# Four output tiles side by side at four stage entries, from weight blocks of two contraction tiles

## The chip, the core and the metric

The kernel runs on one core of one Trainium2 chip. The metric is the device time of one execution in microseconds (us); lower is better. TensorE (PE in the profile) does the matrix products, ScalarE (ACT) and VectorE (DVE) prepare operands and take results out of the PSUM banks, GpSimd (POOL) adds squares for the norms, and SyncE (SP) issues the DMAs. Each engine works through its own list of instructions in order; semaphores hold an instruction until another engine has done what it needs.

## What is computed

The program is two transformer-like blocks on 256 tokens of width 2048, all in float32. Reduced to its large products (`D = 2048`, `T = 256`):

```python
# first block
u = rmsnorm(x, norm_pre)
proj = u @ a_w_in                      # 2048 -> 4096: first half "xb", second half "gate"
xc = causal_conv4(proj[:, :D]) ; r, i = sigmoid(xc @ w_r), sigmoid(xc @ w_i)       # "gates"
y = (linear_recurrence(r, i, xc) * silu(proj[:, D:])) @ a_w_out                    # "aout"
x1 = x + rmsnorm(y, norm_post)
x2 = x1 + sigmoid(x1 @ ple_w_gate) * (p @ ple_w_proj)                              # "pleg", "plep"
# second block
mod = silu(c) @ w_mod + b_mod          # shifts, scales and gains of the norms
um = rmsnorm(x2) * (1 + sc_m) + sh_m
proj = um @ w_in                       # 2048 -> 11264: "cv","cg","i","ff","fb","q","g","gc","gh"
x3 = x2 + ga_m * rmsnorm(merge(conv_branch, hgrn_branch) @ w_out)                  # "wout"
u2 = rmsnorm(x3) * (1 + sc_f) + sh_f
out = x3 + ga_f * rmsnorm(relu(u2 @ mlp_w1) ** 2 @ mlp_w2)                         # "mlp1", "mlp2"
```

A context of 256 further tokens takes part in `i`, `ff` and `fb`; its normed form `uc` is made by the background task `prepare_ctx`.

## The kernel before, in words

**Layout and products.** Activations lie feature-major: 16 feature tiles of 128 partitions by 256 tokens. An output tile is 128 output features by 256 tokens, summed over the 16 tiles of the contraction (`kt` 0 to 15, called k-tiles here). For precision every weight and every activation is split into a high part of reduced width and the remainder. One product of one k-tile into one output tile is three matmuls (high by high, high by low, low by high; every matmul has the line L758), or two wider ones in `mlp1` and `mlp2`.

**Weight blocks.** Weights come from HBM in blocks of 128 x 1024 float32 (512 KB). A block holds 8 k-tiles of one output tile, so a tile takes two blocks. A DMA puts it in one of 7 buffers `WF`; ScalarE writes the high part to one of 4 buffers `WH` (L1015, 128x1024); VectorE writes the low part, `WF` minus `WH`, to `WL` (L1377, 128x1024). ScalarE may overwrite a slot only when PE has done the last product of the block four earlier (semaphore `prod`).

**Order.** `timetable()` writes out one list of steps, and every engine walks that list and does its share of each step. `prepare()` puts the `split` steps (WH, WL) so that PE has them `LA` = 2 blocks ahead. `linear()` runs one output tile: for each half `begin()` (which calls `prepare()`), eight products; then `evac`, in which ScalarE and, for some kinds, VectorE take the tile out of its bank. Four PSUM banks (`GBANKS` = 4) go round; the first product into a bank waits until it was freed (semaphores `free0` to `free3`). Steps of `background` tasks are put between products by `tick()`.

**Stage entries.** At the start of `xb`, `pleg`, `cv` and `mlp1` the activations themselves are only being made: step `make` has VectorE scale one k-tile, ScalarE write its high part and VectorE its low part (L1384 and L1377, 128x256), for `pleg` two k-tiles at a time (128x512). There `linear_pair()` runs two output tiles side by side, so that each k-tile serves both as it appears. Its two tiles need four blocks, in the order first half of both, second half of both. `make` runs some four k-tiles ahead of the products.

**Fills.** The modulation product `mod` (192 blocks, 24 column groups of 8) is spread over the kernel: `modp` steps do it on PE (four 128x512 matmuls a block, line `bank<-WF,SM`), `modv` steps on VectorE (L1384, 128x512). Some `modp` blocks stand before an entry, so that PE has work while a norm is being finished. `close` and `row` steps bring the sums into place.

Of the kernel before, what the change touches and what calls it, by code (L numbers as in the profile page):

```python
# [13 lines left out]
P = 128  # L14
# [41 lines left out]
def timetable():  # L56
# [26 lines left out]

    def add_pair(kind, name, one, two, fill=(0, 0, 0), after=0):


        order.append((kind, (one, two)))
        cg, kp0, kp1 = fill
        ring = [{"of": "w", "name": name, "index": index, "lo": lo} for lo in (0, BLK) for index in (one, two)]
# [4 lines left out]
    add_pair("xb", "a_in", 0, 1)  # L94
    for j in range(1, 8):
        for n in range(2):
            add("xb", "a_in", 2 * j + n)
            if j > 1 or n:
                add_spread()
        if j % 2 == 0:  # L100
            add("gates", "a_gates", j // 2 - 1)
# [9 lines left out]
    for j in range(4):  # L111
        add("plep", "ple_p", j, (0,))
    add_pair("pleg", "ple_g", 0, 1, (1, 0, 8), 4)
    for j in range(2, 16):
        add("pleg", "ple_g", j)
        add_mod(j % 2, 64)
    add_pair("cv", "w_in", 40, 41, (20, 0, 4), 2)
    for t in range(42, 56):
        add("cv" if t < 48 else "cg", "w_in", t)
        add_mod(int(t < 48), 160)  # L120
    for t in range(24):
# [20 lines left out]
    for q in range(4):  # L142
        if q == 0:
            add_pair("mlp1", "mlp1", 0, 1, (20, 4, 8))
        for j in range(2 if q == 0 else 0, 16):
# [134 lines left out]
    def skip():  # L280
        while blocks[st["at"]]["of"] != "w":
            st["at"] += 1
# [12 lines left out]
    def product(what, n, first=True, last=True):  # L295

        at = len(steps)
        for k in range(n):
            steps.append(("prod", what, k, first and k == 0, last and k == n - 1, k == n - 1, st["used"]))
            if k + 1 < n:  # L300
                tick()
        st["prod"] += 1
        return at
# [18 lines left out]

    def linear_pair(kind, js):
        for j in js:
            new_tile((kind, j))
        made = 0
        for h in range(2):
            while made < min(8 * h + 4, KT):
                steps.append(("make", kind, made))
                made += 1  # L330
            begin()
            for k in range(8):
                while made < min(8 * h + k + 5, KT):
                    steps.append(("make", kind, made))
                    made += 1
                for n, j in enumerate(js):
                    steps.append(("prod", (kind, j, h), k, h + k == 0, h == 1 and k == 7, k == 7, st["used"] + n))
            for n in range(2):
                st["prod"] += 1
                skip()  # L340
                end()
        for n, j in enumerate(js):
            tile[(kind, j)].append(st["prod"] - 1 + n)
            steps.append(("evac", (kind, j)))
            if kind in AFTER:
                chains.append([kind, j, 0])
        advance()
# [5 lines left out]
    for kind, j in order:  # L353
        first = kind not in seen
        if kind == "pleg" and first:
            prepare(ahead=NB - 1)
        if first or (kind == "mlp2" and j[1] == 0):
            settle()
        seen.add(kind)
        pair = isinstance(j, tuple) and kind != "mlp2"  # L360
        if kind == "xb":
            if pair:
# [35 lines left out]
        elif kind == "pleg":  # L398
            if pair:
                prepare(fill=8)  # L400
                linear_pair(kind, j)
            else:
                linear(kind, j)
            if j == 5:
                steps.append(("load_ctx",))
            if j == 15:
                steps.append(("warm", 2))
        elif kind == "cv":
            if pair:
# [5 lines left out]
                linear_pair(kind, j)  # L415
                st["stride"] = 4
            else:
                linear(kind, j)
            if j == 42:
                steps.append(("keep",))  # L420
                background.append(("prepare_ctx", 0))
        elif kind == "cg":
            linear(kind, j - 48)
        elif kind == "i":
            if first:
                finish()
                background.append(("conv_branch", 0))
            linear(kind, j)
        elif kind == "ff":
            linear(kind, j - 8)  # L430
        elif kind == "fb":
            if first:
                while background:
                    step()
                background.append(("ctx_decayed", 0))
            linear(kind, j - 16)
        elif kind == "q":
            if first:
                finish()
                background += [("conv_split", 0), ("ctx_decayed", 1), ("ctx_states", 0)]  # L440
                background += [("hgrn", pr) for pr in range(4)]
                beside += [("readout", pr) for pr in range(4)]
            linear(kind, j - 24)
        elif kind == "g":
            if first:
                while ("ctx_states", 0) not in finished:
                    step()
            linear(kind, j - 32)
        elif kind in ("pw", "hout"):
            if kind == "hout" and first:  # L450
                finish()
            linear(kind, j, 1)
        elif kind in ("gc", "gh"):
            linear(kind, j - (56 if kind == "gc" else 72))
            if kind == "gh" and first:
                steps.append(("back",))
        elif kind == "wout":
            if first:
                mods_done(8, 12)
                steps.append(("gains", "wout"))  # L460
                steps.append(("warm", 3))
            linear(kind, j)
        elif kind == "mlp1":
            if pair:
# [11 lines left out]
                linear_pair(kind, j)  # L476
# [29 lines left out]
def build(nc, ctx, ins, out):  # L506
# [247 lines left out]
    def tensor_program(tensor):  # L754
# [11 lines left out]

        def product(what, k, start, stop, inc, n):
            kind, j, h = what
            slot, kt, off = n % NB, 8 * h + k, k * P
            if kind != "gates":  # L770
# [15 lines left out]
            elif kind == "gates":  # L786
                g, b, ri, m = j
                f = 4 * g + 2 * b + k
                hi, lo, off = XCs[:, f % 8, 0, :], XCs[:, f % 8, 1, :], (ri * 2 + k) * T + m * P
                w.wait_ge(xc_lo, f + 1)  # L790
            elif kind == "aout":
                w.wait_ge(ys_lo, kt + 1)
            elif kind == "plep":
                off = k * 512 + (j % 4) * P
                w.wait_ge(ps_lo, k + 1)
            elif kind == "pleg":
# [212 lines left out]
    def scalar_program(scalar):  # L1009
# [65 lines left out]
        def evac(what):  # L1075
# [295 lines left out]
    def vector_program(vector):  # L1371
# [167 lines left out]
        def after(kind, j, n):  # L1539
# [9 lines left out]
            elif kind == "pleg":  # L1549
                s = area(58 + j % 2, 1)[:, 0, :]  # L1550
                w.wait_ge(*left((kind, j)))
# [427 lines left out]
```

## Time and profile before

| what | us |
|---|---|
| median of 3 runs | 2226.75 |
| range of the 3 runs | 2226.0 to 2229.08 |
| the profiled execution, whole | 2226.39 |
| its span in the profile | 2224.6 |
| PE busy in the span | 2135.6 |
| VectorE busy | 1586.5 |
| ScalarE busy | 988.0 |

The page gives for each engine the time in which it was busy. PE leaves 2224.6 - 2135.6 = 89.0 us of the span unused. The other engines have more free time in all, but they work in order and often stand waiting for each other, and where PE waits it is for one of them. Times inside the trace count from the start of the span; 1.8 us of the execution lie outside it.

### The profile page before, as it was taken

What the parts mean: (1) busy time and instruction counts of PE and PEld (TensorE: products, weight loads), DVE (VectorE), ACT (ScalarE), POOL (GpSimd) and SP (SyncE); (2) the same over time, 40 slices, a digit from 0 to 9 for tenths busy, and PEclk for the clock granted to TensorE, in tenths of its full rate; (3) what the DMA queues carried; (4) which work ended last, traced back from release to release, by engine and by line L of the source; (5) the groups of instructions that cost most, each with busy time, mean ns of one, the idle gap of its engine ahead of it and who ended that gap; (6) DMA issues with size and microseconds to landing.
All of it is one profiled execution on the core that took longest, in us unless ns stands there. A gap on an engine that the chain in (4) does not pass through costs nothing.

```text
span 2224.6 us, 33792 instructions
## 1 busy us (share of the span) xinstructions
PE 2135.6 (96%) x14048; PEld 1915.5 (86%) x14048; DVE 1586.5 (71%) x2365; ACT 988.0 (44%) x1494; POOL 52.3 (2%) x61
## 2 busy tenths in 40 slices
PE   6999989999899999999999999989999999999997
PEld 4778889797898788999989999968888888888886
DVE  7667688688769768657676888866675675655665
ACT  5576444445532322444544444444444434434443
POOL 0000002010000000000000000100000000000000
PEclk9999999999999999999999999999999999999998
DMA  5666768575642457533335988945675685555552
GB/s 199 201 197 201 251 225 274 196 268 195 235 154 95 133 197 232 176 124 123 124 116 160 327 310 300 327 138 194 223 265 199 208 264 189 187 192 189 189 180 95
DMA packets 121689, 447.94 MB, mean 201 GB/s; under 512 B 13504, under 2 KB 13760, under 8 KB 121152
## 3 DMA queue, kind: packets, MB, share of 16 engines
q1 hardware_dynamic: 121536, 445.78, 59.6%
q8 instruction: 111, 1.82, 0.3%
q14 instruction: 42, 0.34, 0.0%
HBM read 441.53 MB, written 4.19 MB: 200 GB/s over the span
## 4 chain that ended last, share of the span: by engine, by line
PE 66%; DVE 6%; ACT 2%; issue 1%; DVEq 0%
PE bank L758 66%; DVE AR L1377 2%; DVE WL L1377 1%; DVE AR L1384 1%; DVE AR L1464 1%; ACT WH L1015 1%; ACT AR L1016 0%; DVE SR L1384 0%; PE bank L879 0%; DVE AR L1380 0%; ACT AR L1015 0%; ACT L1016 0%; PE bank L910 0%; DVE AR L1711 0%; ACT SR L1016 0%
## 5 line engine op out<-in xcount | busy, mean ns | idle before, releaser
L758 PE MATMUL bank<-SR,WH 128*128 128x256 f32 (+1 forms) x8128 | 1945.7, 325 | 44.3 <-DVE WL L1377 25.8
L758 PEld LDWEIGHTS bank<-SR,WH 128*128 128x128 f32 x8128 | 1366.6, 192 | 197.0 <-issue 37.1
L758 PE MATMUL bank<-SR,WL 128*128 128x256 f32 (+1 forms) x5088 | 1481.2, 291 | 0.0
L1377 DVE TENSOR_TENSOR WL<-WF,WH 128x1024 fp32r<-128x1024 f32 x636 | 763.8, 1221 | 354.4 <-ACT WH L1015 353.8
L758 PEld LDWEIGHTS bank<-SR,WL 128*128 128x128 f32 x5088 | 974.9, 192 | 15.1
L1015 ACT ACTIVATE WH<-WF 128x1024 fp32r<-128x1024 f32 x636 | 642.8, 1052 | 118.6 <-PE bank L758 110.8
L1384 DVE SCALAR_TENSOR_TENSOR AR<-WF,SM,AR 128x512 f32<-128x512 f32 x345 | 258.6, 771 | 7.8
L1015 ACT ACTIVATE AR<-bank 128x256 f32<-128x256 f32 (+2 forms) x199 | 80.2, 414 | 263.3 <-PE bank L758 249.9
L1015 ACT ACTIVATE SR<-AR 128x256 fp32r<-128x256 f32 (+1 forms) x154 | 64.6, 427 | 296.4 <-DVE AR L1384 177.6
L1016 ACT ACTIVATE AR<-bank 128x256 f32<-128x256 f32 x152 | 56.1, 380 | 284.9 <-PE bank L758 284.6
L1377 DVE TENSOR_TENSOR AR<-AR 128x256 f32<-128x256 f32 (+7 forms) x376 | 165.2, 474 | 18.8 <-ACT AR L1016 14.7
L1377 DVE TENSOR_TENSOR AR<-AR,bank 128x256 f32<-128x256 f32 x112 | 47.1, 421 | 91.9 <-PE bank L758 65.6
L1903 POOL TENSOR_TENSOR AR<-AR 128x256 f32<-128x256 f32 x56 | 51.9, 927 | 2150.8 <-ACT AR L1016 2150.8
L1016 ACT ACTIVATE AR<-AR 128x256 f32<-128x256 f32 (+3 forms) x70 | 42.9, 614 | 121.3 <-DVE AR L1377 57.8
L758 PE MATMUL bank<-AR 128*128 128x128 f32 (+1 forms) x416 | 66.0, 303 | 12.7 <-ACT AR L1015 9.4
L1384 DVE SCALAR_TENSOR_TENSOR AR<-AR,PR 128x256 f32<-128x256 f32 (+12 forms) x168 | 73.8, 442 | 4.8
L1377 DVE TENSOR_TENSOR SR<-AR,SR 128x256 fp32r<-128x256 f32 (+1 forms) x154 | 65.8, 434 | 14.8 <-ACT SR L1015 14.2
L758 PE MATMUL bank<-WF,SM 128*2 128x512 f32 x160 | 73.4, 592 | 0.0
L758 PEld LDWEIGHTS bank<-AR 128*128 128x128 f32 x416 | 57.1, 195 | 16.3 <-ACT AR L1015 10.8
L1377 DVE TENSOR_TENSOR AR<-bank,AR 128x256 f32<-128x256 f32 x80 | 33.6, 420 | 22.8 <-ACT AR L1016 21.8
L758 PEld LDWEIGHTS bank<-WF,SM 128*2 128x2 f32 x160 | 11.2, 84 | 39.4 <-issue 35.9
L1016 ACT ACT_TABLE_LOAD x32 | 41.1, 1283 | 1.3 <-PEq L1970 0.7
(64 smaller groups left out, 451.7 us busy)
## 6 DMA issues: line engine op xcount, KB each, us to landing
WF<-in_mlp SPq DMA_DIRECT2D x256, 512.0 KB, 4.3
WF<-in_mod SPq DMA_DIRECT2D x192, 512.0 KB, 4.9
WF<-in_w_in SPq DMA_DIRECT2D x176, 512.0 KB, 4.3
WF<-in_a_in SPq DMA_DIRECT2D x64, 512.0 KB, 5.0
WF<-in_a_out SPq DMA_DIRECT2D x32, 512.0 KB, 5.1
WF<-in_ple_g SPq DMA_DIRECT2D x32, 512.0 KB, 5.9
WF<-in_w_out SPq DMA_DIRECT2D x32, 512.0 KB, 5.7
WF<-in_pw SPq DMA_DIRECT2D x16, 512.0 KB, 3.5
```

Source lines behind the costliest of these rows:

```text
L758: return tensor.matmul(o, l, r, start=start, stop=stop, skip_group_check=True)
L1015: return scalar.activation(o, x, f, scale=scale)
L1016: return scalar.activation(o, x, f, scale=scale, bias=bias)
L1377: return vector.tensor_tensor(o, a, b, op)
L1384: return vector.scalar_tensor_tensor(o, a, s, b, op1, op2)
L1464: vector.reciprocal(dst, dst).then_inc(st_rs, 1)
L1903: pool.tensor_tensor(ACC, ACC, SQ[ft % 2], ALU.add).then_inc(acc, 1)
```

## The change

- `linear_pair()` becomes `linear_quad()`: at the four entries output tiles 0 to 3 (40 to 43 of `w_in`) run side by side.
- The weights of these four tiles are laid out anew on the host (`beside`): a block now holds k-tiles 2b and 2b+1 for all four tiles. Eight blocks b = 0 to 7 are consumed in turn, each by 8 products. The total of blocks, products and evacuations is the same.
- `make` now runs two to four k-tiles ahead: two `make` steps, a block's split, two `make` steps, the block's products, and so on.
- All four banks are taken by the four tiles. Their four evacuations follow together; in `mlp1` the steps after tiles 0 and 1 are done before tiles 2 and 3 are taken out. For `pleg` the sigmoid has four buffers instead of two.
- The early splits of four blocks before `pleg` and `mlp1` (`prepare(ahead=NB - 1)`) go. In `pleg` three blocks are split ahead of the fills; in `mlp1` two blocks are split while `wout` still runs.
- Some `mod` blocks are given to other tiles, with the same total at each stage.

```diff
-    def linear_pair(kind, js):
+    def linear_quad(kind, js):
         for j in js:
             new_tile((kind, j))
         made = 0
-        for h in range(2):
-            while made < min(8 * h + 4, KT):
+        for b in range(8):
+            while made < min(2 * b + 2, KT):
                 steps.append(("make", kind, made))
                 made += 1
             begin()
-            for k in range(8):
-                while made < min(8 * h + k + 5, KT):
-                    steps.append(("make", kind, made))
-                    made += 1
+            while made < min(2 * b + 4, KT):
+                steps.append(("make", kind, made))
+                made += 1
+            for kk in range(2):
                 for n, j in enumerate(js):
-                    steps.append(("prod", (kind, j, h), k, h + k == 0, h == 1 and k == 7, k == 7, st["used"] + n))
-            for n in range(2):
-                st["prod"] += 1
-                skip()
-                end()
+                    kt = 2 * b + kk
+                    steps.append(("prod", (kind, j), kt, (4 * kk + n) * P, kt == 0, kt == KT - 1, 4 * kk + n == 7,
+                                  st["used"]))
+            st["prod"] += 1
+            end()
         for n, j in enumerate(js):
-            tile[(kind, j)].append(st["prod"] - 1 + n)
-            steps.append(("evac", (kind, j)))
-            if kind in AFTER:
-                chains.append([kind, j, 0])
+            evac((kind, j))
+            if kind == "mlp1" and n == 1:
+                settle()
         advance()
...
-        if kind == "pleg" and first:
-            prepare(ahead=NB - 1)
...
-                prepare(ahead=NB - 1)
                 steps.append(("recip", "x3"))
-                linear_pair(kind, j)
+                linear_quad(kind, j)
...
-                w.wait_ge(x2, j - 1)
-                act(area(58 + j % 2, 1)[:, 0, :], ps, ACT.Sigmoid).then_inc(leave, 1)
+                w.wait_ge(x2, j - 3)
+                act(area(58 + j % 4, 1)[:, 0, :], ps, ACT.Sigmoid).then_inc(leave, 1)
```

**VectorE at the start of `xb`.** `WL` rows are weight blocks, `AR` rows scale a k-tile, `SR` rows write its low part. Before:

```order
L1377 TENSOR_TENSOR WL<-WF,WH 128x1024 [waits w_hi] x2
L1464 RECIPROCAL AR<-AR 128x256 [waits st_sq]
L1384 SCALAR_TENSOR_TENSOR AR<-AR,PR 128x256 [waits st_rs]
L1384 SCALAR_TENSOR_TENSOR AR<-AR,PR 128x256
L1377 TENSOR_TENSOR SR<-AR,SR 128x256 [waits n_hi]
L1384 SCALAR_TENSOR_TENSOR AR<-AR,PR 128x256
L1377 TENSOR_TENSOR SR<-AR,SR 128x256 [waits n_hi]
L1384 SCALAR_TENSOR_TENSOR AR<-AR,PR 128x256 [waits n_lo]
L1377 TENSOR_TENSOR SR<-AR,SR 128x256 [waits n_hi]
L1377 TENSOR_TENSOR WL<-WF,WH 128x1024 [waits w_hi]
```

And now (the file's lines are one lower):

```order
L1376 TENSOR_TENSOR WL<-WF,WH 128x1024 [waits w_hi] x2
L1463 RECIPROCAL AR<-AR 128x256 [waits st_sq]
L1383 SCALAR_TENSOR_TENSOR AR<-AR,PR 128x256 [waits st_rs]
L1383 SCALAR_TENSOR_TENSOR AR<-AR,PR 128x256
L1376 TENSOR_TENSOR SR<-AR,SR 128x256 [waits n_hi]
L1376 TENSOR_TENSOR WL<-WF,WH 128x1024 [waits w_hi]
L1383 SCALAR_TENSOR_TENSOR AR<-AR,PR 128x256
L1376 TENSOR_TENSOR SR<-AR,SR 128x256 [waits n_hi]
L1383 SCALAR_TENSOR_TENSOR AR<-AR,PR 128x256 [waits n_lo]
L1376 TENSOR_TENSOR SR<-AR,SR 128x256 [waits n_hi]
L1376 TENSOR_TENSOR WL<-WF,WH 128x1024 [waits w_hi]
```

The first block's split inside the entry came after four scaled k-tiles and now comes after two; from there on one split follows every two k-tiles, seven before the low part of k-tile 13. In `cv` and `mlp1` it is the same.

**ScalarE at the start of `pleg`.** `SR` rows write the high part of two k-tiles, `WH` rows are weight blocks. Before:

```order
L1015 ACTIVATE WH<-WF 128x1024 [waits landed5]
L1015 ACTIVATE WH<-WF 128x1024 [waits landed6]
L1015 ACTIVATE SR<-AR 128x2x256 [waits ds_x] x6
L1015 ACTIVATE WH<-WF 128x1024 [waits prod,landed1]
L1015 ACTIVATE SR<-AR 128x2x256 [waits ds_x] x2
```

And now:

```order
L1014 ACTIVATE WH<-WF 128x1024 [waits landed5]
L1014 ACTIVATE SR<-AR 128x2x256 [waits ds_x] x2
L1014 ACTIVATE WH<-WF 128x1024 [waits landed0]
L1014 ACTIVATE SR<-AR 128x2x256 [waits ds_x]
L1014 ACTIVATE WH<-WF 128x1024 [waits prod,landed1]
L1014 ACTIVATE SR<-AR 128x2x256 [waits ds_x]
L1014 ACTIVATE WH<-WF 128x1024 [waits prod,landed2]
L1014 ACTIVATE SR<-AR 128x2x256 [waits ds_x]
L1014 ACTIVATE WH<-WF 128x1024 [waits prod,landed3]
```

The fourth block moved behind the second pair of k-tiles, and from the fourth pair on each pair stands behind a block that waits for PE (`prod`).

**PE where the tiles side by side end in `mlp1`.** `bank` numbers are the tiles' banks. Before:

```order
L758 MATMUL bank0<-SR,WH 128x512 [waits n_lo]
L758 MATMUL bank0<-SR,WL 128x256
L758 MATMUL bank1<-SR,WH 128x512
L758 MATMUL bank1<-SR,WL 128x256
L758 MATMUL bank2<-SR,WH 128x512 [waits free2,w_lo]
```

And now:

```order
L758 MATMUL bank0<-SR,WH 128x512 [waits n_lo]
L758 MATMUL bank0<-SR,WL 128x256
L758 MATMUL bank1<-SR,WH 128x512
L758 MATMUL bank1<-SR,WL 128x256
L758 MATMUL bank2<-SR,WH 128x512
L758 MATMUL bank2<-SR,WL 128x256
L758 MATMUL bank3<-SR,WH 128x512
L758 MATMUL bank3<-SR,WL 128x256
L758 MATMUL bank0<-SR,WH 128x512 [waits free0,w_lo]
```

The next tile went into bank 2, which had long been free; it now goes into bank 0, whose last product is seven matmuls back.

## Rows read from the trace of the kernel before

**Rows 1.** The page: busy time by engine, and the costliest group of matmuls
```profile
PE 2135.6 (96%) x14048; PEld 1915.5 (86%) x14048; DVE 1586.5 (71%) x2365; ACT 988.0 (44%) x1494; POOL 52.3 (2%) x61
...
L758 PE MATMUL bank<-SR,WH 128*128 128x256 f32 (+1 forms) x8128 | 1945.7, 325 | 44.3 <-DVE WL L1377 25.8
```
**Rows 2.** Stretches: engines' busy us (instructions), clock, DMA share, GB/s
```profile
450.00:500.00 50.00, 50.00 (x419) 50.00 (x419) 41.18 (x56) 23.38 (x36) 6.67 (x9) 1.00 0.78 274
580.00:602.00 22.00, 16.99 (x132) 15.77 (x130) 15.41 (x27) 12.13 (x20) 0.00 (x0) 1.00 0.46 155
434.00:437.00 3.00, 2.93 (x13) 2.77 (x14) 2.00 (x4) 1.61 (x2) 0.00 (x0) 0.53 0.07 26
```
**Rows 3.** Timeline of the xb entry: start, us, engine, operation [idle before <-releaser]
```profile
19.47 0.88 DVE L1384 SCALAR_TENSOR_TENSOR AR<-AR,PR 128x256 f32<-128x256 f32 x2
...
23.42 1.23 DVE L1377 TENSOR_TENSOR WL<-WF,WH 128x1024 fp32r<-128x1024 f32 x1 [1.09 <-ACT WH L1015]
...
24.56 0.48 DVE L1384 SCALAR_TENSOR_TENSOR AR<-AR,PR 128x256 f32<-128x256 f32 x1
...
26.02 0.48 DVE L1384 SCALAR_TENSOR_TENSOR AR<-AR,PR 128x256 f32<-128x256 f32 x1
...
46.11 1.88 PE L758 MATMUL bank<-WF,SM 128*2 128x512 f32 x4
...
53.86 1.88 PE L758 MATMUL bank<-WF,SM 128*2 128x512 f32 x4
```
**Rows 4.** Timeline, VectorE in cg, where the context is normed: two weight blocks
```profile
592.56 1.23 DVE L1377 TENSOR_TENSOR WL<-WF,WH 128x1024 fp32r<-128x1024 f32 x1 [1.40 <-ACT WH L1015]
...
596.50 1.23 DVE L1377 TENSOR_TENSOR WL<-WF,WH 128x1024 fp32r<-128x1024 f32 x1 [1.13 <-ACT WH L1015]
```
**Rows 5.** Timeline of the cv entry, VectorE and PE
```profile
526.15 0.88 DVE L1384 SCALAR_TENSOR_TENSOR AR<-AR,SM 128x256 f32<-128x256 f32 x2
...
530.41 1.23 DVE L1377 TENSOR_TENSOR WL<-WF,WH 128x1024 fp32r<-128x1024 f32 x1 [1.13 <-ACT WH L1015]
...
540.38 0.79 PE L758 MATMUL bank<-SR,WH 128*128 128x256 f32 x2 [3.25 <-DVE WL L1377]
...
556.31 0.50 PE L758 MATMUL bank<-SR,WH 128*128 128x256 f32 x2
```
**Rows 6.** Timeline of the mlp1 entry, VectorE, PE and ScalarE
```profile
1476.32 4.62 DVE L1377 TENSOR_TENSOR WL<-WF,WH 128x1024 fp32r<-128x1024 f32 x4
...
1482.64 0.88 DVE L1384 SCALAR_TENSOR_TENSOR AR<-AR,SM 128x256 f32<-128x256 f32 x2
...
1499.03 0.74 ACT L1015 ACTIVATE AR<-bank 128x256 f32<-128x256 f32 x2 [1.25 <-PE bank L758]
...
1508.21 0.50 PE L758 MATMUL bank<-SR,WH 128*128 128x512 f32 x1
```
**Rows 7.** Timeline of the pleg entry, VectorE, ScalarE and PE
```profile
423.22 0.51 PE L758 MATMUL bank<-SR,WH 128*128 128x256 f32 x2
...
424.00 1.41 DVE L1377 TENSOR_TENSOR AR<-AR 128x512 f32<-128x512 f32 x2
...
426.72 1.41 DVE L1377 TENSOR_TENSOR AR<-AR 128x512 f32<-128x512 f32 x2
...
428.98 1.06 ACT L1015 ACTIVATE WH<-WF 128x1024 fp32r<-128x1024 f32 x1 [0.18 <-PE bank L758]
...
431.21 1.41 DVE L1377 TENSOR_TENSOR AR<-AR 128x512 f32<-128x512 f32 x2
...
434.07 0.71 PE L758 MATMUL bank<-SR,WH 128*128 128x256 f32 x2 [1.95 <-DVE SR L1377]
...
447.80 0.50 PE L758 MATMUL bank<-SR,WH 128*128 128x256 f32 x2
...
457.49 3.23 DVE L1384 SCALAR_TENSOR_TENSOR AR<-WF,SM,AR 128x512 f32<-128x512 f32 x4
```
**Rows 8.** Waits of PE from 559 to 610 us: total, times, longest
```profile
PE bank L758 <- DVE WL L1377: 6.4, 6, 2.5
```

More of the change, by code:

```diff
@@ L82, in add_spread, with add_quad @@
                            "last": i % 8 == 7})
-    def add_pair(kind, name, one, two, fill=(0, 0, 0), after=0):
-        order.append((kind, (one, two)))
+    def add_quad(kind, name, one, fill=(0, 0, 0), after=0):
+        order.append((kind, tuple(range(one, one + 4))))
         cg, kp0, kp1 = fill
-        ring = [{"of": "w", "name": name, "index": index, "lo": lo} for lo in (0, BLK) for index in (one, two)]
+        ring = [{"of": "w", "name": name, "index": one + b // 2, "lo": b % 2 * BLK} for b in range(8)]
         ring[after:after] = [{"of": "p", "name": "mod", "index": 8 * cg + kp, "lo": 0, "fill": True,
@@ L92, in add_pair @@
         blocks.extend(ring)
-    add_pair("xb", "a_in", 0, 1)
-    for j in range(1, 8):
+    add_quad("xb", "a_in", 0)
+    for j in range(2, 8):
         for n in range(2):
             add("xb", "a_in", 2 * j + n)
-            if j > 1 or n:
+            add_spread()
+            if j == 2:
                 add_spread()
@@ L112, in timetable @@
         add("plep", "ple_p", j, (0,))
-    add_pair("pleg", "ple_g", 0, 1, (1, 0, 8), 4)
-    for j in range(2, 16):
+    add_quad("pleg", "ple_g", 0, (1, 0, 8), 3)
+    for j in range(4, 16):
         add("pleg", "ple_g", j)
-        add_mod(j % 2, 64)
-    add_pair("cv", "w_in", 40, 41, (20, 0, 4), 2)
-    for t in range(42, 56):
+        add_mod(j % 2 + int(j == 4), 64)
+    add_quad("cv", "w_in", 40, (20, 0, 4), 2)
+    for t in range(44, 56):
         add("cv" if t < 48 else "cg", "w_in", t)
-        add_mod(int(t < 48), 160)
+        add_mod((1 + t % 2) * int(t < 48), 160)
     for t in range(24):
@@ L143, in timetable @@
         if q == 0:
-            add_pair("mlp1", "mlp1", 0, 1, (20, 4, 8))
-        for j in range(2 if q == 0 else 0, 16):
+            add_quad("mlp1", "mlp1", 0, (20, 4, 8), 2)
+        for j in range(4 if q == 0 else 0, 16):
             add("mlp1", "mlp1", 16 * q + j)
@@ L298, in product @@
         for k in range(n):
-            steps.append(("prod", what, k, first and k == 0, last and k == n - 1, k == n - 1, st["used"]))
+            kind, j, h = what
+            off = k * 512 + j % 4 * P if kind == "plep" else (j[2] * 2 + k) * T + j[3] * P if kind == "gates" else k * P
+            steps.append(("prod", (kind, j), 8 * h + k, off, first and k == 0, last and k == n - 1, k == n - 1,
+                          st["used"]))
             if k + 1 < n:
@@ L359, in timetable @@
         seen.add(kind)
-        pair = isinstance(j, tuple) and kind != "mlp2"
+        quad = isinstance(j, tuple) and kind != "mlp2"
         if kind == "xb":
-            if pair:
-                linear_pair(kind, j)
+            if quad:
+                linear_quad(kind, j)
                 background.append(("small_params", 0))
@@ L398, in timetable @@
         elif kind == "pleg":
-            if pair:
+            if quad:
                 prepare(fill=8)
-                linear_pair(kind, j)
+                linear_quad(kind, j)
             else:
@@ L408, in timetable @@
         elif kind == "cv":
-            if pair:
+            if quad:
                 mods_done(0, 8)
@@ L418, in timetable @@
                 linear(kind, j)
-            if j == 42:
+            if quad:
                 steps.append(("keep",))
@@ L463, in timetable @@
         elif kind == "mlp1":
-            if pair:
+            if quad:
                 steps.append(("stat", "y2"))
@@ L765, in both, with product @@
             return bass.AP(tensor=X.tensor, offset=X.offset, ap=[X.ap[0], [32 * KB, 2], [1, T]])
[L767 to L769 removed]
+        def product(what, kt, off, start, stop, inc, n):
+            kind, j = what
+            slot = n % NB
             if kind != "gates":
@@ L1936, in tiles, with beside @@
             w.reshape(k // P, P, n // cols, cols).transpose(2, 1, 0, 3).reshape(n // cols, P, -1))
+    def beside(w, one):
+        four = w[one:one + 4].reshape(4, P, 4, 2, 2, P).transpose(2, 1, 3, 4, 0, 5).reshape(4, P, 2048)
+        return np.concatenate([w[:one], four, w[one + 4:]])
     vec = {
@@ L1961 @@
             a["w_mod_2"][0].reshape(8, 2, P, 24, 512).transpose(3, 0, 2, 1, 4).reshape(192, P, BLK)),
-        "w_in": tiles(a["w_in_2"][0], P),
+        "w_in": beside(tiles(a["w_in_2"][0], P), 40),
         "pw": tiles(a["conv_pw_w_2"][0], P),
@@ L1965 @@
         "w_out": tiles(a["w_out_2"][0], P),
-        "mlp1": tiles(a["mlp_w1_2"][0], P),
+        "mlp1": beside(tiles(a["mlp_w1_2"][0], P), 0),
         "mlp2": np.ascontiguousarray(
```

18 lines of the change are left out of this document (9 added, 9 removed).

## The prediction

> **What bounds the kernel now.** First the busy times: PE works 2135.6 of 2224.6 us, and the idle time in front of its main group of matmuls is put down mostly to VectorE's weight blocks [rows 1]. The change keeps every matmul, so it can only touch the 89.0 us in which PE idles, and the time it loses at the lower clock. Then the stretches: at full clock 419 matmuls take 50.0 us, 0.119 us each [rows 2]. So one product (three matmuls) is 0.36 us, a k-tile for four tiles 1.43, a block of two k-tiles for four tiles 2.87. Last the timelines of the four entries, where the question is who sets the pace: PE's 2.87 us a block, or VectorE and ScalarE, who must make two k-tiles and split one block in that time.
>
> **The pace inside the new entries.** In `xb` two k-tiles cost VectorE 26.02 - 24.56 = 1.46 us; a block's low part takes 24.56 - 23.42 = 1.14; and before it VectorE stands 1.09 us, since ScalarE does the block's high part only after the high part of the newest k-tile [rows 3]. The new order has exactly this, two k-tiles and then a split, every time: 1.46 + 1.09 + 1.14 = 3.69 us a block. For `cv` and `mlp1` the trace has the very sequence (two scales, two low parts, one split) where the context is normed: 596.50 - 592.56 = 3.94 us [rows 4]. Both are longer than 2.87. So VectorE sets the pace inside all four entries, PE idles about 1 us a block, and the ring of four blocks can't help. What the change gains against this is that PE has four tiles to fill, where before it stood for whole blocks of time.
>
> **xb.** Scaling begins at 19.47 as before. The first block's low part began at 23.42 behind four scaled k-tiles [rows 3]; two fewer put it at 23.42 - 1.46 = 21.96. The seventh begins 6 x 3.69 later, 44.1. The low part of k-tile 13 is ready 1.9 us after that (1.14, then a scale and a low part), 46.0, and three k-tiles (13, 14, 15) of 1.43 follow: 50.3. Before, four tiles and one `mod` block (1.8) were done at 53.86 [rows 3], so without the block at 52.05. Gain 1.75. PE then has two `mod` blocks, 3.6 us, from another bank, while tile 0's bank is freed; the wait for banks is hidden there, and costs about 2 us if it isn't. VectorE's twelve operations on the four tiles and the small parameters end before PE needs their blocks. **-1.7**, between -3.5 and +0.5.
>
> **pleg.** Here VectorE makes two k-tiles in 426.72 - 424.00 = 2.72 us, and 431.21 - 426.72 = 4.49 with a split between, of which 0.18 was ScalarE waiting for PE [rows 7]. I take 4.3, with 4.49 as the other end. Before, the fills on PE ended at 423.22, where the pair began. The fifth block of the entry may be written only when PE has done the first, at 423.22 + 2.87 = 426.1. Behind that wait stand, in ScalarE's order, the high parts of k-tiles 6 and 7, and so all that follows. With 1.05 + 1.14 for the block, pair 3 of k-tiles (6 and 7) is scaled from 428.4, pair 7 from 428.4 + 4 x 4.3 = 445.6, and its low part is ready 2.75 later, 448.3. PE's last block ends at 451.2. Before, the last half tile began at 447.80 [rows 7] and ended at 450.7. So the entry ends 0.5 us later, although before PE stood 1.95 us and then ran 3 us at clock 0.53 [rows 2, 7]. Tile 4 must wait for bank 0: the matmul's end and one sigmoid, 0.45. Behind it VectorE owes a `mod` block (3.2 us) [rows 7], four tiles' additions (4 x 0.84) and the next splits; ScalarE's squares of these tiles stand ahead of its next block. By that count the second block of tile 5 comes at 460.7 instead of 460.3, and after the next `mod` block the first of tile 6 at 465.1 instead of 463.7: 0.4 + 1.4. **+2.8**, between 0 and +5.
>
> **cv.** The first split goes from behind four k-tiles to behind two, 530.41 - 1.58 = 528.8 [rows 5]; the seventh starts at 528.8 + 6 x 3.94 = 552.5, k-tile 13 is ready 2.1 later, and PE ends at 554.6 + 4.3 = 558.9. Before, the last half of tile 3 began at 556.31 [rows 5] and ended at 559.2. The long wait of 3.25 us is gone, and eight short ones have come. Tile 4 waits 0.45 for its bank. Then the context is normed beside `cg`, where PE already waits 6.4 us for weight blocks [rows 8]. That task starts one tile later and keeps its work and its two `mod` blocks, so I leave the 6.4 as they are; they are the largest unknown: shared work behind the entry could add or save some 3 us. **+0.1**, between -3.5 and +3.5.
>
> **mlp1.** Four splits of 4.62 us stood on VectorE between the norm's sum and its scaling [rows 6]. Two are now done under `wout`, where VectorE idles, and two inside the entry, so that scaling starts at 1482.64 - 4.5 = 1478.15. This is the change's best term, but the pace eats it: the first split at +2.7, 1480.85, the seventh at 1504.5, k-tile 13 at 1506.6, the end at 1510.9. Before, the last half began at 1508.21 [rows 6] and ended 2.87 later, at 1511.1. Gain 0.2. Then the bank: one copy on ScalarE (half of 0.74) [rows 6], an addition of 0.42 on VectorE and the hand-overs, 0.95. **+0.75**, between -0.5 and +2.5.
>
> The Trainium skill (Perfetto Trace Analysis, Optimizing Tensor Performance, Matmuls) says independent groups of matmuls should rotate through the banks, so that one's evacuation lies under the next one's products. The quad gives that up for one hand-over at each entry. The trace of before shows PE going on without a gap at these places, in line with the rule; by it the three uncovered hand-overs are a loss, which the sums above hold as 0.45, 0.45 and 0.95 from their own rows.
>
> **Sum.** -1.7 + 2.8 + 0.1 + 0.75 = +1.95 us against the profiled execution of 2226.39 (span 2224.6 and 1.8 around it): 2228.3. The median lies 0.36 above that execution, so I say **2228.7**. Repeated measurement of this kernel can tell about 0.2%, 4.5 us.
>
> **Rivals.**
> *Faster.* The work behind the entries fits better than counted: no stalls in `pleg` behind tile 4 (-1.8), the bank waits half as long (-0.9), and the waits beside the context's norm fall by half because the mod sums lie before them (-3.2). That is 2228.7 - 5.9 = 2222.8, and with the low end of `xb` 2221. For it: VectorE is free a quarter of the time. Against: its free time is nearly all waiting for ScalarE in the same order.
>
> *Slower, the backlog.* In `pleg` the block that waits for PE holds back k-tiles, and `mod` sums, additions and squares of four tiles come at once behind it. It decides from the point where VectorE's debt at the end of the quad passes the two blocks that PE has in hand, 5.7 us; I count 3.2 + 3.4 + 2.3 = 8.9 in the first tile and a half. If this also happens in `cv` before the context's norm (+3) and `pleg` is at its +5: 2228.7 + 5.2 = 2234.
>
> *Slower, the clock.* At 434.07, after 1.95 us idle, the granted clock was 0.53 [rows 2, 7]; from 580 to 602 us, with PE busy 17.0 of 22.0 us and gaps near 1 us, it stayed 1.00 [rows 2]. The quads in `xb`, `cv` and `mlp1` look like the latter (2.87 of 3.7 to 3.94 busy, 73 to 78%); `pleg`'s is thinner, 2.87 of 4.3, 67%, with gaps of 1.4. At half speed a block takes 5.74 us, 1.44 over the pace of 4.3. If the clock fell for the last five blocks of `pleg`: +7, 2236; in all four entries 8 x 1.8 three times more, 2279. The Trainium skill (TensorE: Matmul & The Clock Gate, A second HAM failure mode: psum-queue depth-cycling) tells of a kernel whose short idles between groups of matmuls made the clock swing. By that rule this rival would win; the stretch from 580 us speaks against it.
>
> *Nothing done.* The four blocks hold all tiles' weights and the order shows them used; that it does not do what it says I exclude.
>
> **How the numbers follow.** The forecast, within 0.2% of before (2222.3 to 2231.2), has 0.60. The backlog 0.20 and the clock 0.08, both slower; the faster case 0.12. The range leaves out the clock and half of the faster case: 2222 to 2236. Faster by over 0.2%: 0.13. Within: 0.59. Slower: 0.28.
>
> **What would show it.** Inside the quads VectorE's weight blocks at a pitch of 3.7 us in `xb`, 3.9 in `cv` and `mlp1`, 4.3 in `pleg`, each but pleg's behind some 1.1 us of waiting for `WH`, and PE idle 0.6 to 1.2 us before most blocks, at clock 1.00. PE's first product of `mlp1` some 4.5 us after the gains, not 9. A gap of 0.5 us at banks in `pleg` and `cv`, about 1 in `mlp1`, none in `xb`. Two stalls at tiles 5 and 6 of `pleg`. The context's waits again near 6.4. The prediction is wrong if VectorE's pitch is below 3 us (ScalarE would then have done the high parts early), if the clock falls inside a quad, or if the waits beside the context's norm change by more than 3 us.

## The result, and the profile after

| | before | changed kernel |
|---|---|---|
| median | 2226.65 us | 2233.44 us |
| range of 9 runs | 2226.0 to 2229.08 | 2228.36 to 2240.23 |
| ratio to before, 95% interval | | 1.0032, 1.0017 to 1.0048 |
| the profiled execution, whole | 2226.39 | 2238.40 |
| its span | 2224.6 | 2236.6 |

The change costs about 0.3%. The forecast was 2228.7 us with a range of 2222 to 2236, and its likeliest case was "within 0.2%", 2222.3 to 2231.2. The median lies in the range, but 4.7 us above the forecast and 2.2 above the end of that case; what came is the case "slower by over 0.2%", which had 0.28. The scatter is new as well: 3 us before, 12 us now, and four of the nine executions lie above 2236.

The page of the changed kernel answers to [rows 1]: busy times, and the group of PE's main matmuls.

```profile
PE 2142.6 (96%) x14048; PEld 1913.2 (86%) x14048; DVE 1589.2 (71%) x2365; ACT 986.5 (44%) x1494; POOL 48.8 (2%) x61
...
L758 PE MATMUL bank<-SR,WH 128*128 128x256 f32 (+1 forms) x8128 | 1951.4, 326 | 47.1 <-DVE WL L1376 18.6
```

PE idles 2236.6 - 2142.6 = 94.0 us instead of 89.0. But the 14048 matmuls are also 7.0 us longer busy, and none was added or changed in shape. So the 12 us have two sources, and the second has nothing to do with waits.

**Where the 12 us are.** Both kernels run the same matmuls in nearly the same order, so the start of the n-th matmul can be set against the same one before. How much this difference grew over each stretch:

| stretch | forecast | changed kernel | the same kernel profiled again |
|---|---|---|---|
| start of the first matmul | 0 | +0.6 | +1.2 |
| xb's quad | -1.7 | -1.5 | -1.5 |
| rest, up to the fills before pleg | 0 | -1.5 | -3.1 |
| pleg | +2.8 | +3.4 | +3.4 |
| cv's quad and two tiles behind it | +0.1 | +0.9 | +0.9 |
| beside the context's norm | 0 | +1.6 | +1.6 |
| from there to the fills before mlp1 | 0 | +0.1 | 0.0 |
| mlp1's entry | +0.75 | +1.9 | +1.8 |
| steady mlp1 and mlp2 | 0 | +6.5 | -2.1 |
| sum | +1.95 | +12.0 | +2.2 |

Between these two executions the entries repeat to 0.1 us. The line behind xb's quad doesn't: in two kernels of the experiments that have pairs in xb (low_later_before and quad_in_mlp1_alone), lines two and three together came to -0.1 and -3.2 (short stretches at the lower clock fall in or out), so what stands there beyond the quad is no effect of the change. The last line is the largest difference in the table.

The line of xb needs two remarks. Of its -1.5, 0.4 us arose between the first matmul and the quad's first product; from that product on it is -1.1, in this and in all four other traces with the same quad. And it is measured against one execution of the pair. In the two kernels just named the granted clock fell inside xb's pair, as this row of low_later_before shows, and the pair took 1.4 us longer:

```profile
36.00:40.00 4.00, 4.00 (x27) 4.00 (x26) 2.06 (x6) 1.11 (x3) 0.00 (x0) 0.73 0.49 149
```

Against those the quad's gain would be 2.5 us.

**Inside the quads** it went as forecast. First VectorE's weight blocks in xb, against [rows 3] (timeline: start, us, engine, operation, idle before and what ended it):

```profile
33.36 1.23 DVE L1376 TENSOR_TENSOR WL<-WF,WH 128x1024 fp32r<-128x1024 f32 x1 [1.10 <-ACT WH L1014]
...
37.15 1.23 DVE L1376 TENSOR_TENSOR WL<-WF,WH 128x1024 fp32r<-128x1024 f32 x1 [1.10 <-ACT WH L1014]
```

PE's restarts there:

```profile
35.37 0.50 PE L758 MATMUL bank<-SR,WH 128*128 128x256 f32 x2 [0.65 <-DVE SR L1376]
39.16 0.51 PE L758 MATMUL bank<-SR,WH 128*128 128x256 f32 x2 [0.66 <-DVE SR L1376]
```

VectorE's weight blocks in cv, against [rows 4, 5]:

```profile
537.48 1.23 DVE L1376 TENSOR_TENSOR WL<-WF,WH 128x1024 fp32r<-128x1024 f32 x1 [1.13 <-ACT WH L1014]
...
541.42 1.23 DVE L1376 TENSOR_TENSOR WL<-WF,WH 128x1024 fp32r<-128x1024 f32 x1 [1.13 <-ACT WH L1014]
```

The pitch is 3.79 us in xb (forecast 3.69), 3.94 in cv and in mlp1 (3.94), 4.20 in pleg (4.3). PE stands idle 0.65 us in xb, waiting for a k-tile's low part, since VectorE stands 1.10 us in front of every weight block. In pleg VectorE stands 0.25 us before a block and 0.70 before the low part of a pair of k-tiles. PE's restarts in pleg, from the quad to the tiles behind it:

```profile
437.66 0.47 PE L758 MATMUL bank<-SR,WH 128*128 128x256 f32 x2 [1.10 <-DVE SR L1376]
...
449.73 0.48 PE L758 MATMUL bank<-SR,WH 128*128 128x256 f32 x2 [0.56 <-ACT AR L1015]
459.47 0.50 PE L758 MATMUL bank<-SR,WH 128*128 128x256 f32 x2 [0.87 <-DVE WL L1376]
463.26 0.51 PE L758 MATMUL bank<-SR,WH 128*128 128x256 f32 x2 [0.66 <-DVE WL L1376]
```

The same in mlp1, from its first product on:

```profile
1483.41 0.76 PE L758 MATMUL bank<-SR,WH 128*128 128x512 f32 x1 [4.53 <-DVE SR L1383]
...
1515.88 0.47 PE L758 MATMUL bank<-SR,WH 128*128 128x512 f32 x1 [1.02 <-DVE AR L1376]
1524.83 0.50 PE L758 MATMUL bank<-SR,WH 128*128 128x512 f32 x1 [0.38 <-DVE WL L1376]
```

At 449.73 is the wait for bank 0, at 459.47 and 463.26 the stalls in tile 5 and at tile 6 of pleg that the prediction named. In mlp1 the first product now waits 4.5 us instead of 9, the bank costs 1.0, and a further 0.4 follows.

**The clock** stayed up inside the quads, but for the start of mlp1's. Stretches of pleg, cv and mlp1, columns as in [rows 2]:

```profile
430.00:447.00 17.00, 13.20 (x106) 12.49 (x106) 13.06 (x17) 7.63 (x10) 0.00 (x0) 1.00 0.37 124
526.00:556.00 30.00, 25.17 (x171) 20.45 (x170) 22.14 (x39) 14.95 (x24) 0.00 (x0) 1.00 0.52 167
1483.00:1486.50 3.50, 3.09 (x9) 2.44 (x10) 2.64 (x6) 1.59 (x3) 0.00 (x0) 0.52 0.06 9
1486.50:1513.00 26.50, 21.54 (x115) 17.13 (x115) 19.00 (x34) 13.74 (x21) 0.00 (x0) 1.00 0.40 138
```

Behind its wait of 4.5 us PE begins mlp1 at the lower of its two levels (0.5 of full speed); the pair before did so too, behind 9.1 us. From there on the gaps of 0.85 us leave the clock at 1.00.

**Beside the context's norm** PE's waits for weight blocks between 559 and 625 us come to 7.7 us, against 6.4 in [rows 8]; no such wait falls between 610 and 625 before:

```profile
PE bank L758 <- DVE WL L1376: 7.7, 7, 2.5
```

**The pitch of the steady part.** Two stretches of 100 us in mlp1 and mlp2, PE never idle in them and at clock 1.00, first in the kernel before:

```profile
1800.00:1900.00 100.00, 100.00 (x579) 88.15 (x578) 64.66 (x87) 41.74 (x53) 0.00 (x0) 1.00 0.66 218
1900.00:2000.00 100.00, 100.00 (x579) 88.19 (x578) 60.50 (x82) 41.87 (x53) 0.00 (x0) 1.00 0.56 192
```

and in the changed one:

```profile
1800.00:1900.00 100.00, 100.00 (x567) 86.67 (x567) 64.42 (x86) 40.57 (x49) 0.00 (x0) 1.00 0.65 219
1900.00:2000.00 100.00, 100.00 (x567) 86.67 (x566) 60.16 (x84) 42.53 (x55) 0.00 (x0) 1.00 0.56 190
```

579 matmuls in the one, 567 in the other: 346.7 ns for a product of two matmuls against 353.3. Over the 976 products between two breaks in the stream that is 6.5 us. These 976 run from the second quarter's mlp2 tiles to the last mlp1 tile, over half of them in mlp1; the expectations below call the whole "mlp2's long stretch".

### The profile page after: what moved, and what is told of

It is laid out like the page before. It is cut to its first block, busy times and chain, and to the rows that moved or that the text cites. A ratio compares the mean times of both kernels' runs of the same rounds, so it can differ in the third digit from the quotient of the medians.

```text
span 2236.6 us, 33825 instructions
## 1 busy us (share of the span) xinstructions
PE 2142.6 (96%) x14048; PEld 1913.2 (86%) x14048; DVE 1589.2 (71%) x2365; ACT 986.5 (44%) x1494; POOL 48.8 (2%) x61
## 4 chain that ended last, share of the span: by engine, by line
PE 65%; DVE 6%; ACT 2%; issue 1%; DVEq 0%; ACTq 0%
PE bank L758 65%; DVE AR L1376 2%; DVE WL L1376 1%; ACT WH L1014 1%; DVE AR L1383 1%; DVE AR L1463 1%; ACT AR L1015 0%; ACT AR L1014 0%; PE bank L878 0%; DVE SR L1383 0%; ACT L1015 0%; ACT SR L1015 0%; PE bank L909 0%; DVE AR L1710 0%; DVE AR L1379 0%
```

## The experiments

**The changed kernel again, unedited.**

> The changed kernel once more, unchanged, to see its own scatter. In its trace the long stretch of mlp2 (matmuls 11576 to 13528 of the order, 339 us before, 345 us after) went at 353.3 ns a product against 346.7 ns before, which is 6.5 of the 12 us between the two profiled executions. Theory A (the pitch of that stretch falls on one of two values from run to run): the times again spread over two groups some 6 to 9 us apart, and a profiled execution at 346.7 ns ends near 2229 to 2232, one at 353.3 ns near 2238. Rival B (the change itself sets the slower pitch): every execution of this kernel has 353.3 ns there, and the groups come from elsewhere.

Measured: 2234.23 us, 2228.61 to 2238.68 (6 runs), ratio 1.0034 (1.0021 to 1.0048). The profiled execution took 2228.61, and its row for 1800 to 1900 us reads

```profile
1800.00:1900.00 100.00, 100.00 (x579) 88.22 (x578) 64.57 (x87) 41.27 (x51) 0.00 (x0) 1.00 0.65 219
```

So theory A holds where it matters: the same program has either pitch. (The six times do not fall into two clear groups; other stretches change their pitch too.) It also ran the stretch from 1540 to 1640 us at 581 matmuls where the other two have 569; over the part with that pitch this is worth another 2.1. Both together are 8.6 of the 9.8 us between the two executions of this kernel.

**A pair in pleg, quads elsewhere.**

> The changed kernel with the old pair, its early split of four blocks and its order of mod blocks in pleg alone; xb, cv and mlp1 stay quads. By the traces pleg grew by 3.4 us (2.7 of it in the first tile and a half behind the quad). Theory: the stage from its first fill to the start of cv is 3 to 4 us shorter than in the changed kernel, and xb, cv and mlp1 are unchanged to 0.5 us. Rival (the loss behind the quad comes from what stands before pleg and is only late there): under 1 us. The whole time can hide it behind the scatter of mlp2.

Measured: 2232.63 us (2229.35 to 2235.19, 8 runs). From the fills to the start of cv the stage is 0.4 us shorter than before, 3.8 shorter than the changed kernel's; xb's quad (from its first product on), cv and mlp1 repeat to 0.1. The theory holds. The 0.4 is the clock: PE idles the same 1.95 us in this pair as in the kernel before, but the clock stays up behind it, where [rows 2] has 0.53:

```profile
434.00:437.00 3.00, 2.33 (x19) 2.33 (x20) 0.62 (x1) 2.14 (x4) 0.00 (x0) 1.00 0.02 5
```

**The low part later, inside the quads.** ScalarE walks the list as before. VectorE does a block's low part two k-tiles further on. As a sketch of the list of steps for one block (not the lines of the file):

```diff
-    split(b + 2)
-    make(2b + 2)
-    make(2b + 3)
+    high(b + 2)
+    make(2b + 2)
+    make(2b + 3)
+    low(b + 2)
```

where `high` is ScalarE's half of `split` and `low` is VectorE's. In pleg `low` stands between the sums of a pair of k-tiles and their low part.

> The changed kernel with one move in VectorE's order, inside the four quads only: the low part of a weight block stands behind the two k-tiles that are made next (in pleg behind the sums of the next pair and ahead of its low part), while ScalarE does the high part where it did. No instruction is added. Theory (VectorE stood 1.13 us per block because ScalarE did the block's high part only behind the newest k-tile): the wait goes, VectorE's pitch falls from 3.79 (xb) and 3.94 (cv, mlp1) to 2.6 to 2.8 us, under PE's 2.87, and from 4.20 to 3.3 in pleg; PE's gaps between blocks (0.8 in xb, 0.96 in cv, 0.9 in mlp1) vanish, worth 4 + 4 + 5.8 + 5.5 = 19 us, of which I expect 14 to 19 at the end: 2214 to 2219 (6 more if mlp2 falls on its slow pitch). Rival (the ring of four blocks or PE's bank hand-over takes over as the bound): the pitch stays above 3.4 and the gain is under 5 us.

Measured: 2213.49 us (2207.05 to 2220.86, 6 runs), ratio 0.994 (0.9922 to 0.9958). VectorE in xb:

```profile
33.94 1.22 DVE L1419 TENSOR_TENSOR WL<-WF,WH 128x1024 fp32r<-128x1024 f32 x1
...
36.82 1.22 DVE L1419 TENSOR_TENSOR WL<-WF,WH 128x1024 fp32r<-128x1024 f32 x1
```

VectorE, and the one restart of PE, in cv:

```profile
527.00 1.22 DVE L1419 TENSOR_TENSOR WL<-WF,WH 128x1024 fp32r<-128x1024 f32 x1
...
529.72 1.22 DVE L1419 TENSOR_TENSOR WL<-WF,WH 128x1024 fp32r<-128x1024 f32 x1
...
544.60 0.48 PE L801 MATMUL bank<-SR,WH 128*128 128x256 f32 x2 [0.56 <-ACT AR L1057]
```

No idle time stands ahead of the blocks any more, the pitch is 2.88 in xb, PE's own pace, and 2.72 in cv, and PE's only idle time from 520 to 550 us is the bank's 0.56. By stretches, against the kernel before: xb's quad -6.1, pleg -1.1, cv -5.6, mlp1 -5.0, that is 4.6, 4.5, 6.5 and 6.9 us less than the changed kernel, 22.5 in all, more than the 14 to 19 expected. One move of VectorE's half of a step turns a loss into a gain of 0.6%; this execution even had the pitch of 353.3 ns.

**The same beside the context's norm.**

> The same, and the same move for the eight weight blocks beside the context's norm in cv and cg, where PE waited 6.4 us in the kernel before and VectorE stood 1.13 to 1.40 us per block behind ScalarE. Theory: those waits of PE go but for the one behind the activation table, 4 to 6 us less than low_later. Rival (the weight blocks there come late for another reason, the mod sums ahead of them): under 1.5 us less.

Measured: 2205.24 us (2198.49 to 2214.47, 6 runs), ratio 0.9908 (0.9888 to 0.9927). The stretch beside the norm is 7.0 us shorter than in low_later, more than the 4 to 6 expected, and one wait of PE is left there:

```profile
570.61 0.80 PE L801 MATMUL bank<-SR,WH 128*128 128x256 f32 x2 [2.34 <-DVE WL L1419]
...
575.00:600.00 25.00, 25.00 (x211) 25.00 (x210) 19.65 (x31) 15.11 (x23) 0.00 (x0) 1.00 0.59 198
```

It is not the one that was expected to stay. The load of the activation table (1.28 us) stands at 577.75 us here, and PE is never idle from 575 to 600: that wait, 2.49 us in low_later, is gone, and the expectation had not counted it. What is left is the first wait of the stretch, and it grew from 0.75 to 2.34. VectorE works through a mod block for 3.2 us just ahead, and the move put the weight block's low part behind two more k-tiles:

```profile
564.67 3.17 DVE L1426 SCALAR_TENSOR_TENSOR AR<-WF,SM,AR 128x512 f32<-128x512 f32 x4
...
569.34 1.22 DVE L1419 TENSOR_TENSOR WL<-WF,WH 128x1024 fp32r<-128x1024 f32 x1
```

So the move costs something where a mod block precedes it; a version that leaves this one block where it was wasn't tried.

**This move alone, in the kernel before.**

> The kernel before, pairs everywhere, with nothing changed but VectorE's place for the low parts of the weight blocks beside the context's norm (as in low_later_ctx). Theory (those waits have nothing to do with the quads): the stretch from the end of cv's four tiles to the first quarter of the i stage is 6 to 7 us shorter, 2219.5 to 2221, with times close together. Rival: the gain needs the mod blocks where the quads' version has them, under 3 us.

Measured: 2219.66 us (2219.23 to 2223.05, 7 runs), ratio 0.997 (0.996 to 0.9981). The stretch is 6.6 us shorter. The wait was there before the change and needed no quad to go.

**Pairs with the better order.**

> What the four tiles side by side are worth by themselves once VectorE's order is mended: pairs in all four entries, their splits spread evenly (one block per four k-tiles where the early ones don't cover it) and every low part behind the next two k-tiles, in the entries and beside the context's norm, as in low_later_ctx. A pair needs a k-tile every 0.72 us on PE and VectorE gives four k-tiles and one block in 4.06, so VectorE still sets the pace until the sixteenth k-tile; a quad needs four of them in 5.7. Theory: each entry ends 2 to 4 us later than the quad's, in all 2205.2 + 12 = 2214 to 2221. Rival (the four tiles bring nothing, all the gain was in the order): within 3 us of 2205.

Measured: 2212.68 us (2212.11 to 2213.53, 5 runs), ratio 0.9938 (0.9926 to 0.995), so 7.4 us over low_later_ctx (the kernel before, measured beside each, 2226.9 and 2226.3), where 9 to 16 were expected. Against the pairs' stretches the quads win 3.8 in xb, 4.5 in cv and 3.0 in mlp1, and lose 1.4 in pleg and 1.2 beside the context's norm. The 12 us were too many because I had counted pleg as a win and the stretch beside the norm as even. The 3.0 is low: in low_later_ctx mlp1 began with the clock at 0.50 from 1458.5 to 1464.5 us, which took 1.1 more than the start in low_later; in low_later, low_later_ctx_mods and best its entry is 4.9 to 5.0 us shorter than before, against 0.9 with the pair. So the quad is worth something, though in pleg it never was.

**A pair in mlp1, and a quad in mlp1 alone.**

> The changed kernel with the old pair and its early splits in mlp1 alone; xb, pleg and cv stay quads. By the traces mlp1's entry grew by 1.9 us (start of the products 4.5 earlier, the quad 4.5 longer, banks 1.2 and 0.8), and behind it mlp2's long stretch fell on 353.3 ns a product in some executions and on 346.7 ns in others, where the kernel before has shown 346.7 alone. Theory A (what the quad leaves behind in mlp1 sets on which pitch mlp2 falls): with the pair back the times lie close together again, as the kernel before's, near 2226 to 2228, and the profile shows 346.7. Theory B (any shift of some us does it): the times spread over 6 us or more as the changed kernel's do, with a lowest near 2226.5.

> The counterpart: pairs in xb, pleg and cv as in the kernel before, a quad in mlp1 alone. Theory A: lowest time near 2228.3 (2226.4 + 1.9), others 6 to 9 us above it, spread as the changed kernel's. Theory B: spread too, so this run alone does not tell them apart, but its stage gives mlp1's own term: from the last fills before mlp1 to the steady stretch 1.9 us longer than before.

Measured: with the pair 2229.59 us (2227.87 to 2231.01, 11 runs), with only mlp1's quad 2228.98 (2224.92 to 2235.54, 12 runs). Three microseconds of spread against eleven speak for theory A, and the profile with the pair shows 346.7. Its median missed the expected 2226 to 2228. The other's lowest time, 2224.9, lies 3.4 below the expected one; in that execution 3.3 had been gained before mlp1, where nothing was changed. Mlp1's entry is 0.1 us shorter than before in the one and 1.9 longer in the other, as forecast from the traces.

**Mod sums moved off the tiles behind pleg's quad.**

```diff
-        add_mod(j % 2 + int(j == 4), 64)
+        add_mod(int(j in (6, 7, 8, 9, 11, 13, 15)), 64)
```

> low_later_ctx with the mod block that VectorE sums right behind pleg's quad (with tile 4) given to tile 6, and the odd tile 5's to tile 8; the total is the same. In every trace with a quad PE stood 1.15 and 0.93 us at tiles 5 and 6 of pleg. Theory (backlog: mod sums, additions and splits come at once): both stalls go or fall under 0.3 us, 1.5 to 1.9 us less than low_later_ctx, by the stage from the quad's end to tile 7; the banks' 0.7 us stays. Rival (ScalarE's squares of four tiles hold the block back): the stalls stay, under 0.5 us less.

Measured: 2201.5 us (2199.42 to 2204.27, 4 runs), ratio 0.9891 (0.9877 to 0.9906). Its median is 3.7 us under low_later_ctx's, but the scatter of mlp1 and mlp2 lies in that; the stage alone tells. PE's waits behind the quad:

```profile
440.21 0.48 PE L801 MATMUL bank<-SR,WH 128*128 128x256 f32 x2 [0.56 <-ACT AR L1058]
449.94 0.50 PE L801 MATMUL bank<-SR,WH 128*128 128x256 f32 x2 [0.86 <-DVE WL L1419]
```

The stall at tile 6 is gone, the one in tile 5 is as it was: 0.8 us of the 1.5 to 1.9 expected. Ahead of that block VectorE works through the eight additions of the four tiles (4.2 us), and ScalarE through their squares. The backlog was half mod sums, half the four tiles' own work.

**The last block tile by tile.**

```diff
+            if b == 7:
+                turns.sort(key=lambda t: t[1])
```

> The changed kernel with one move on PE: the eight products of a quad's last block run tile by tile (both k-tiles of tile 0, then of tile 1, and so on), so that tile 0 is complete 5 products, 1.8 us, ahead of the quad's last one, and its bank can be emptied beside the other three. Theory: PE's waits for the bank right behind the quads go, 0.72 in pleg, 0.72 in cv and 1.18 in mlp1; xb has none to lose. In pleg the stall behind it may take the 0.7 back. In all 1.2 to 2.6 us less than the changed kernel at equal pitches of mlp2. Rival (the wait ends with something other than the bank, ScalarE's or VectorE's order): under 0.5 us.

Measured: 2236.23 us (2230.44 to 2239.76, 5 runs), and the waits for the banks behind the quads (0.56, 0.56 and 1.02 us of idling) unchanged to 0.01 us. The expectation was wrong, for a reason that stands in the code: `evac` waits for the count of blocks that PE has finished, and that count rises with the last product of the block. Tile 0 was complete earlier, but ScalarE was told no earlier. A signal of its own for each tile wasn't tried.

**Everything together, and the same with a pair in mlp1.**

> All that helped together: low parts later in the quads and beside the context's norm, pleg's mod sums moved off the tiles behind the quad, last block tile by tile. Theory: the terms add, low_later_ctx_mods less 1.2 to 2.6: lowest 2197, median 2198 to 2201; 6.5 more in executions in which mlp2's long stretch falls on 353.3 ns. Rival: no less than 2201.5.

> The same with a pair in mlp1 (its splits spread evenly, low parts later). Theory: mlp1's quad is worth 3.9 us by the traces plus 1.2 by its last block, so this is 4 to 5 us slower than the best's quick executions, 2201.5 to 2203, but with times within 2 us of each other, since behind a pair every trace so far showed 346.7 ns in mlp2's long stretch. Rival (the scatter comes from elsewhere): spread of 6 us or more.

Measured: 2205.0 us (2198.69 to 2207.89, 5 runs), ratio 0.9899 (0.9884 to 0.9914), and 2205.4 us (2203.07 to 2206.28, 4 runs), ratio 0.9904 (0.989 to 0.9917). The profiled execution of the first took 2205.01 and had 568 matmuls from 1800 to 1900 us; less 6.5 it is 2198.5. The median misses the expected 2198 to 2201. Since the last block's order does nothing, this is low_later_ctx_mods over again, and the two share their range. mlp1's entry is 3.9 us shorter with the quad (-5.0 against -1.1), which the slower pitch takes back in some executions: in the median the pair is as good, though 4 to 5 us slower were expected of it, and its spread is 3 us instead of 9.

Every version with the low part later beats both kernels. I would keep low_later_ctx_mods: its four executions lie about 1.1% under the kernel before, and together with the five of best, which do the same work, about 1.0%.

## Why the prediction was right and wrong

*What bounds the kernel, and the pace of the quads: right.* VectorE's pitch, PE's idle 0.6 to 1.1 us before most blocks and the 4.5 us at the start of mlp1 came out to 0.1 us of their terms, and the clock stayed up but for mlp1's first products (0.52), where VectorE set the pace anyway. The argument that the sequence "two k-tiles, then a split" already stands beside the context's norm was the one that carried the forecast. The Trainium skill (TensorE: Matmul & The Clock Gate, A second HAM failure mode: psum-queue depth-cycling) tells of a kernel whose short idles between groups of matmuls made the clock swing. That did not happen here: the rows above show 1.00 with PE idle up to 1.1 us per block.

*xb: right in kind, the gain forecast a little large* (-1.1 from the first product on, for -1.7). *pleg: right in kind, the loss forecast a little small* (+3.4 for +2.8). Of the pair's time in the trace of before, which both numbers are set against, 0.4 belonged to a fall of the clock that three other traces of that pair don't show. The quad's end was +0.6 for +0.5, the stalls in tiles 5 and 6 together 2.05 for 1.8. The bank took 0.72 of PE's time, not 0.45: the next matmul starts 0.85 us behind the start of the last one, where 0.12 is usual, and 0.28 of that is the matmul and 0.56 the copy with its hand-over.

*cv: the step that failed is "so I leave the 6.4 as they are".* The waits beside the norm grew by 1.3 us and by one in number, 1.6 with what lies between, and the bank took 0.7 here too. The task began one tile later, and behind 610 us it made PE wait for two weight blocks (0.97 and 0.81 us) that had been in time before. I had named this as the largest unknown, but priced its middle at nothing.

*mlp1: a term was mis-sized.* The bank was 1.18 for 0.95, the quad ended level with the pair instead of 0.2 earlier, and I had not looked for what came behind it (0.7, with PE idle at 1524.83), though I had looked for the same in pleg.

*The sum: a term was missing.* The entries made -1.5 + 3.4 + 2.5 + 1.9 = +6.3 us, where the forecast had +1.95, and the third line of the table took some back. That alone would have been 2230 to 2233, between the likeliest case and the backlog rival. What made the profiled execution 2238.4 was the pitch of mlp1 and mlp2, in a stretch that the sum leaves out, since no instruction in it changes. The range was made for other things than this one; that the median still fell into it is in part luck.

*The rivals.* The backlog rival was the nearest, at somewhat over half of its price: 0.6 of 2.2 us in pleg and 2.4 of 3 in cv and behind it. The faster rival was dismissed with the words that VectorE's free time "is nearly all waiting for ScalarE in the same order". Of the 638 us that VectorE is free before, its waits in front of weight blocks are indeed over half:

```profile
DVE WL L1377 <- ACT WH L1015: 353.8, 233, 6.0
```

low_later shows that this was the most valuable sentence in the text: the 1.1 us were not the price of the quad but of one place in a list.

## What to carry to other kernels

When two engines hand work to each other and a third waits, don't only read which one is busy: look at what each does while it waits, and whether the thing waited for could have been asked for one step earlier. Here the high part was made behind the newest k-tile and used at once; letting its user come two k-tiles later took VectorE's wait of 1.1 us a block out of xb, cv and mlp1 and brought 22.5 us in the four entries, with no instruction added. A restructuring that is judged before such a wait is gone is judged by the wait: in the medians four tiles side by side lost 7 us in the old order and gained 7 in the new one.

## What the hardware showed that I had not expected

**A busy TensorE has two pitches.** In mlp1 and mlp2 a product (a matmul of 512 columns and one of 256) takes 346.7 or 353.3 ns, at clock 1.00 and never idle, and keeps that value for 90 to 340 us. Past the first tiles of mlp1 it changed only where four small matmuls (`bank<-CN,AR`) stand in the stream. At 346.7 every product is like the next; at 353.3 the spacing repeats every three products (232 and 118, 241 and 120, 236 and 113 ns). Of the 14 profiled executions, the 5 with a pair in mlp1 (before, pair_in_mlp1, pairs_low_later_ctx, low_later_before, best_pair_in_mlp1) all had 346.7 in the longest stretch; of the 9 with a quad there 4 had 346.7 and 5 had 353.3. The runs' spread agrees: 1.4 to 3.8 us in the four such kernels of the experiments, 4.9 to 16 us in the others, and 5.2 us over all 60 executions of the kernel before that are on record, 2223.9 to 2229.1. That mlp1's entry has a hand in it is therefore likely; what decides in a single execution stays open, and nothing here shows the mechanism.

**Behind the same idle time the clock fell in one execution and not in another.** PE idled 1.95 us at the same place of pleg's pair in four traces. Behind it the granted clock was 0.53 in the kernel before [rows 2, 7] and 1.00 in pair_in_pleg, low_later_before and quad_in_mlp1_alone. In xb's pair PE idled 3.10 us both in the kernel before, where the clock stayed at 1.00, and in quad_in_mlp1_alone, where it was 0.83 from 36 to 40 us. In the quads of xb, pleg and cv, which idled up to 1.10 us every 4.2 us, it fell in no trace. A stretch at the lower clock in one trace is therefore not yet a property of the kernel, and a stage measured against it (0.4 us in pleg, 1.4 in xb) can move by as much.
